# Eight matmuls of the rounded weights first, then the eight of their remainders, in the gate and up products of a float32 transformer kernel

## The reference, cut to what matters

```
h = rms_norm(x, g_ffn_pre[i])
gu = h @ w_gate_up[i]
f = (silu(gu[..., :D_FF]) * gu[..., D_FF:]) @ w_down[i]
x = x + rms_norm(f, g_ffn_post[i])
```

## Time and profile before

| | |
|---|---|
| time, median of 3 (lowest, highest) | 1671.17 us (1670.74, 1676.05) |
| the profiled execution: time, span | 1675.97 us, 1674.1 us |
| TensorE matmuls: busy, count | 1625.9 us (97% of the span), 9616 |
| VectorE, ScalarE busy | 1078.3 us (64%), 878.1 us (52%) |
| TensorE's part of the chain that ended last | 90% of the span |
| matmuls of lines 1810 and 1812 | 2112 each |
| mean granted TensorE clock | 0.992 |

### The profile page before, as it was taken

The page is one execution under the profiler, slowest core; times in us unless marked ns, Lnnn a source line. Parts: engine busy times, 40 slices in busy tenths (PEclk is TensorE's granted clock), DMA queues, the critical chain, the costliest instruction groups (busy, mean ns, idle before and its releaser), DMA issues.

```text
span 1674.1 us, 24383 instructions
## 1 busy us (share of the span) xinstructions
PE 1625.9 (97%) x9616; PEld 1375.4 (82%) x9616; DVE 1078.3 (64%) x1333; ACT 878.1 (52%) x1303; POOL 86.5 (5%) x156
## 2 busy tenths in 40 slices
PE   9999999999999999999998999999999999999997
PEld 9868888986788878888986788888888887688886
DVE  6767656686766666565657565657565666665655
ACT  6555444665544455444657554445444556554442
POOL 1000000040000011000002000002000002000000
PEclk9999999999999999999999999999999999999999
DMA  8325555642455557555440355557555442055551
GB/s 287 126 76 176 180 196 180 197 139 76 155 186 189 187 184 211 197 177 200 156 147 2 101 180 196 178 199 218 202 184 190 162 151 77 3 195 198 182 193 59
DMA packets 202956, 271.70 MB, mean 162 GB/s; under 512 B 4824, under 2 KB 175440, under 8 KB 202880
## 3 DMA queue, kind: packets, MB, share of 16 engines
q1 hardware_dynamic: 200016, 263.39, 46.8%
q0 software_dynamic: 2544, 7.09, 1.7%
q10 hardware_dynamic: 320, 0.18, 0.0%
HBM read 269.58 MB, written 1.05 MB: 162 GB/s over the span
## 4 chain that ended last, share of the span: by engine, by line
PE 90%; DVE 4%; ACT 4%; issue 1%; DMA 0%; POOL 0%; DVEq 0%; POOLq 0%; SPq 0%; ACTq 0%
PE pair L1810 30%; PE pair L1812 15%; PE bank L1743 11%; PE bank L1745 11%; PE bank L1744 11%; PE bank L1959 1%; PE bank L1989 1%; ACT probs L851 1%; PE pair L1939 1%; PE pair L1743 1%; PE pair L1745 1%; PE pair L1744 1%; PE bank L1886 1%; DVE w_lo L1070 1%; ACT w_hi L719 1%
## 5 line engine op out<-in xcount | busy, mean ns | idle before, releaser
L1810 PE MATMUL pair<-xt,w_hi 128*128 128x512 f32 x2112 | 754.7, 401 | 2.1 <-DVE xt L1079 1.9
L1070 DVE TENSOR_TENSOR w_lo<-raw,w_hi 128x2048 fp32r<-128x2048 f32 x248 | 567.6, 2290 | 145.9 <-ACT w_hi L719 145.0
L719 ACT ACTIVATE w_hi<-raw 128x2048 fp32r<-128x2048 f32 x248 | 473.8, 1914 | 269.8 <-PE pair L1812 200.8
L1812 PE MATMUL pair<-xt,w_lo 128*128 128x256 f32 x2112 | 595.2, 282 | 0.0
L1810 PEld LDWEIGHTS pair<-xt,w_hi 128*128 128x128 f32 x2112 | 399.8, 189 | 102.2 <-issue 3.7
L1812 PEld LDWEIGHTS pair<-xt,w_lo 128*128 128x128 f32 x2112 | 402.0, 190 | 2.3
L1743 PE MATMUL bank<-w_hi,hid_hi 128*128 128x512 f32 x528 | 207.4, 393 | 0.0
L1745 PE MATMUL bank<-w_lo,hid_hi 128*128 128x512 f32 x528 | 206.5, 391 | 0.0
L1744 PE MATMUL bank<-w_hi,hid_lo 128*128 128x512 f32 x528 | 205.9, 390 | 0.0
L1119 DVE TENSOR_TENSOR gate_sum<-pair,gate_sum 128x512 f32<-128x512 f32 x66 | 45.7, 692 | 208.1 <-ACT gate_sum L797 208.1
L1743 PE MATMUL bank<-w_hi,xt 128*128 128x256 f32 (+1 forms) x544 | 163.0, 300 | 0.4 <-DVE xt L1079 0.4
(11 more groups left out here) (277 smaller groups left out, 1579.6 us busy)
## 6 DMA issues: line engine op xcount, KB each, us to landing
raw<-in_w_gate_up SPq DMA_DIRECT2D x44, 1024.0 KB, 5.1
raw<-in_ffn_wg SPq DMA_DIRECT2D x44, 1024.0 KB, 5.1
raw<-in_ffn_wu SPq DMA_DIRECT2D x44, 1024.0 KB, 5.2
raw<-in_ffn_wd SPq DMA_DIRECT2D x44, 1024.0 KB, 5.0
raw<-in_w_in SPq DMA_DIRECT2D x30, 1024.0 KB, 5.3
raw<-in_w_down SPq DMA_DIRECT2D x22, 1024.0 KB, 5.0
raw<-in_w_o SPq DMA_DIRECT2D x8, 1024.0 KB, 5.0
raw<-in_w_out SPq DMA_DIRECT2D x8, 1024.0 KB, 5.0
```

The costliest lines, as they stand in the source:

```text
L719: act.activation(w_hi[s][:, :], raw[s][:, :], ACT.Copy).then_inc(hi_ready, 1)
L1070: dve.tensor_tensor(w_lo[s][:, :], raw[s][:, :], w_hi[s][:, :].bitcast(F32), ALU.subtract)\
L1810: pe.matmul(out[:, 512 * m:512 * (m + 1)], w[0][:, c, cols], xt[:, 2 * SEQ * c:2 * SEQ * (c + 1)], start=(c == 0), stop=False)
L1812: last = pe.matmul(out[:, 512 * m + SEQ:512 * (m + 1)], w[1][:, c, cols], hi_half(xt, c), start=False, stop=(c == KC - 1))
```

## The change

Within each bank, all eight matmuls with `w_hi` are issued first, then all eight with `w_lo`. The unit begins once `w_hi` is there; the wait for `w_lo` moves behind the eight first matmuls of bank 0. Instructions, shapes, operands and the number of weight loads stay the same.

```diff
-                    pe.wait_ge(lo_ready, u + 1 + 6 * i)
+                    pe.wait_ge(hi_ready, u + 1 + 6 * i)
                     w = [v[s][:, :].rearrange("p (c n) -> p c n", c=KC) for v in (w_hi, w_lo)]
                     for m in range(2):
+                        cols = slice(P * m, P * (m + 1))
                         for c in range(KC):
                             if first and m == 0 and c % 2 == 0:
                                 pe.wait_ge(turned_lo.sem, turned_lo.at((pieces, c // 2)))
-                            cols = slice(P * m, P * (m + 1))
                             pe.matmul(out[:, 512 * m:512 * (m + 1)], w[0][:, c, cols],
                                       xt[:, 2 * SEQ * c:2 * SEQ * (c + 1)], start=(c == 0), stop=False)
+                        if m == 0:
+                            pe.wait_ge(lo_ready, u + 1 + 6 * i)
+                        for c in range(KC):
                             last = pe.matmul(out[:, 512 * m + SEQ:512 * (m + 1)], w[1][:, c, cols],
                                              hi_half(xt, c), start=False, stop=(c == KC - 1))
```

## The result

The median fell from 1672.96 us (13 executions, 1670.21 to 1677.86) to 1666.93 us (13 executions, 1665.31 to 1669.11). The ratio is 0.9957, with a 95% interval of 0.9947 to 0.9968: 0.43% faster, or 7.2 us (5.3 to 8.9). The medians alone are 6.0 us apart. The forecast was 11.5 us faster; its wide range of 1656 to 1675 holds the time, its own range of 1656 to 1665 does not.

What follows compares the result with a forecast made beforehand. TensorE, busy 97% of the span, was taken as the bound. Banks -9.7, opening groups -0.9, down units -3.0 and first banks +2.1 sum to -11.5 us: 1671.17 to 1659.7, say 1660 us; range 1656 to 1675, forecast's own 1656 to 1665.

Steps and rivals of the forecast that it cites:

- The wait: Before L1810, relaxing the wait on lo_ready was claimed to be worth nothing.
- (a): Banks of the gate and up groups: 2.78 us a bank instead of 2.82; 54 groups after down units give -9.7 us.
- the entry: Extra time on changing from 256 to 512 columns, taken as 0.01 us from the down unit at 449.62.
- The opening groups: Twelve groups opening the blocks: some seven already quick win nothing, five slow ones give -0.9 us.
- the rival of 0.04: Rival, chance 0.18: entry is 0.04 us, as at 978.52; -3.3 us in all, 1667.9 us.
- (b): Down units: first eight matmuls take 1.82 instead of 1.87 us, -3.0 us over 60 units.
- (c): First bank of each block, while xt pieces arrive: bank 1 0.72 us late in blocks four to six, +2.1 us.
- (d): Work following TensorE: splits and loads stay hidden with 6.8 us to spare, bank copies move along; cost nothing.
- The full entry: Rival, chance 0.24: every bank pays the 0.06 us entry in full; +2.2 us, 1673.4 us, no measurable change.
- hide its loads: Rival, chance 0.05: in each bank's second half, 256-column runs can't hide weight loads; +137 us, 1808 us.
- The clock in the first bank of block four: Rival, chance 0.05: clock falls in first banks of blocks four to six, +10.2 us; near 1670 us with the gain.

Runs made afterwards that it cites:

- the wait alone: Against the kernel before: old matmul order, but units start on w_hi and the w_lo wait stands before its first matmul; ratio 0.9995.
- runs of two: Against the kernel with two-and-two only in the first bank: two matmuls of 512 columns, then two of 256, in every bank; 1660.76 us, timed again 0.9921 of before.
- runs of four: Against the kernel with two-and-two in the first bank: four matmuls of 512 columns, then four of 256, in all other banks; 1668.19 us.
- pairs of two: Against the changed kernel: in each block's first bank only, two w_hi matmuls alternate with two w_lo; ratio 0.9945 of before, median 1664.98 us.
- the order alone: Against the changed kernel: new matmul order kept, the single wait of before restored; ratio 0.9958 of before.
- one entry: Against the kernel with two-and-two in the first bank: later groups issue 18 matmuls of 512 columns, 32 of 256, 14 of 512; 0.9917 of before, again 0.9913.

## Why the prediction was right, and where its size was off

**The wait** was put at nothing, and the experiment with the wait alone shows nothing (0.9995).

**(a) The banks.** The mechanism held: a settled matmul of 512 columns costs 0.2267 us (taken as 0.226), one of 256 costs 0.120, the first bank behind a down unit has no entry, and with all sizes equal the order does nothing. The picture behind it, a price for each change of size, is too simple all the same: runs of two beat runs of four and of eight. What was mis-sized is the entry, "the 0.01 of the down unit at 449.62". It measured 0.03 (1.84 us for eight), near the 0.04 of the other down unit in the earlier trace rows, which I had made a rival. 54 groups gave 54 x (11.146 - 11.290) = -7.8 us in place of -9.7. The choice rested on the thought that a run of 256 is settled and so a clean start. But the down unit at 449.62 follows a slow group of pairs; the one at 978.52 follows a quick group and was the better neighbour. The rival's own sum, -3.3 us, came out too small, since its 11.20 a group took 0.04 a bank where 0.03 was paid, and gave nothing for the first matmuls of a run of 256. So the measured gain lies about midway between the forecast's and this rival's.

**The opening groups** were put at -0.9 us, the quick ones at nothing. This term failed. In the one profiled execution of each kernel, of the six second groups of a block, those of blocks one and two take 11.50 us before (438.12 to 449.62) and those of blocks three to six 11.29 (967.24 to 978.52); both ends stand in the earlier trace rows, the starts are

```profile
438.12 0.58 PE L1810 MATMUL pair<-xt,w_hi 128*128 128x512 f32 x1
...
967.24 0.58 PE L1810 MATMUL pair<-xt,w_hi 128*128 128x512 f32 x1
```

After, all six take 11.36. Two gain 0.14 each and four lose 0.08 each: nothing together. What follows bank 0 in the first groups of blocks four to six adds nothing either: 8.32, 8.48 and 8.32 us before, 8.38 each after. A group whose pairs already ran at the settled sum can only lose by an entry, as the rival of 0.04 had it.

**(b) The down units** take 5.467 us after, and 5.499 in the mean before: 60 x -0.031 = -1.9 us, forecast -3.0, by the same mis-sized entry.

**(c) The first bank** was right in place and size: bank 1 begins 0.72, 0.72 and 0.71 us later, counted from the last piece, in blocks four, five and six, and pairs of two bring it back. At the lower clock nothing was lost, as forecast: the third block began at 0.50 in both profiles, and in the profile after, from its second matmul on, the first eight of 512 columns start 0.427 us from each other, so none of them stood still for a piece. But the clock doesn't fall in every execution. In the profile after the second block began at 1.00, and there, too, bank 1 begins 1.58 us after the last piece. That case had no price in the forecast.

**(d)** No wait on a weight block appeared; the cover of 6.8 us held.

Together -7.8 - 1.9 + 2.1 = -7.6 us. The measured gain is 7.2 us with an interval of 5.3 to 8.9, or 6.0 by the medians; the sum lies within it, and the first groups of blocks one to three, which hang on the clock, are not in it. The absolute forecast of 1660 us also stood on a median of three, 1671.17, where thirteen executions gave 1672.96: 1.8 of the 7 us that it missed by.

**The rivals.** The full entry did not come (0.03, not 0.06). A run of 256 columns does hide its loads: 0.120 in runs of 8 and of 32. The clock in the first bank of block four stayed up; in the profiled execution of the order alone the second block again ran at 0.50 from 419.80 to 426.50, so the missing fall in the profile after isn't the order's doing. By the Trainium skill's gap of N / 2.4 + 2.5 ns (TensorE: Matmul & The Clock Gate, Back-to-back issue gap) the order could change nothing. The runs differ on both counts: a settled fp32r matmul of 512 columns costs 0.2267 us where the rule gives 0.2158, and the spacing does depend on the size of the matmul before.

**What stays open** is what in TensorE makes the entry. Equal sizes exclude the alternation of weight blocks and the sums into fresh columns as causes by themselves; the entry of 0.04 beside 384 columns makes a stream as short as 256 an unlikely condition. And a change of size at every matmul is not enough to cost anything: the same order of 512 and 256 columns ran at 0.347 a pair in the quick groups and at 0.353 behind each of the 54 down units. What decides between the two rhythms, no experiment here tried.

## What to carry to other kernels

When TensorE is full, read the distance from start to start for each size in a settled run and in the loop at hand; where the loop costs more than the sum of the settled prices and mixes sizes, try grouping equal sizes, across banks too. The prize is small: 0.4% here for the change, 0.9% for the best version. Before moving work behind a wait, look at what it filled: here the remainder's matmuls had been filling the time between arriving pieces, and the better versions keep short runs where pieces arrive. Try several run lengths, since the gain isn't monotone.

## What the runs showed of the hardware that I had not expected

- Alternating 512 and 256 columns costs 0.353 us a pair behind a down unit (54 of 54 groups), yet 0.347 in the quick opening groups. In runs of two it costs 11.14 / 32 = 0.348, in runs of four 0.350, in runs of eight 0.348, with one entry 0.347; the settled prices add up to 0.347.
- With 512 and 512 columns alternation costs nothing: 0.2267 each in both orders.
- Behind 256 columns, a run of 512 needs five matmuls to settle and costs 27.5 ns more than settled; behind 512 columns, a run of 256 gives 7.5 ns back.
- With 512 and 384 columns runs of eight are no shorter than pairs (13.02 and 13.00 us a group); 384 columns come down to 0.173 us only at the end of a run of eight.
